# A decoder step with 32 experts: expert weights fetched in 2 MB pieces with 16 KB runs, and turns of the end part moved forward

## What is computed

```python
D_MODEL = D_FF = 1024; N_EXPERTS = 32; TOP_K = 4
SWIGLU_LIMIT = 7.0; SWIGLU_ALPHA = 1.702

def expert_block(args):            # xb: a block of the tokens of expert e
    xb, e = args
    gu = xb @ w_gu[e] + b_gu[e]    # w_gu[e] is 1024 x 2048: 8 MB
    gate, up = gu[:, :D_FF], gu[:, D_FF:]
    gate = jnp.minimum(gate, SWIGLU_LIMIT)
    up = jnp.clip(up, -SWIGLU_LIMIT, SWIGLU_LIMIT)
    hmid = (up + 1.0) * gate * jax.nn.sigmoid(SWIGLU_ALPHA * gate)
    return hmid @ w_down[e] + b_down[e]   # w_down[e] is 1024 x 1024: 4 MB
# y = for each token the sum of its 4 experts' rows, weighted by the gates
# x = x + y;  output = rmsnorm(x, norm_final)
```

## Time and profile before

| | |
|---|---|
| median of 3 runs | 1305.01 us (1304.98 to 1307.53) |
| the profiled execution's own time | 1306.43 us |
| its span, first to last instruction | 1304.7 us |
| granted TensorE clock, mean | 0.995 of full speed |
| bytes moved | 450.56 MB |
| experts' part, first bias matmul to the end | 355.25 to 1304.7 us |

### The profile page before, as it was taken

How to read it: one execution, slowest core, us unless ns; L and a number is a source line. 1 busy time by engine, 2 the same in 40 slices (tenths; PEclk the granted TensorE clock), 3 DMA queues, 4 the chain that set the end, 5 groups by cost and what they waited for, 6 DMA issues and landing times.

```text
span 1304.7 us, 19058 instructions
## 1 busy us (share of the span) xinstructions
PE 1258.8 (96%) x7105; PEld 544.9 (42%) x7105; DVE 474.7 (36%) x990; ACT 199.9 (15%) x347; POOL 65.2 (5%) x146
## 2 busy tenths in 40 slices
PE   7999989989899999999999999999999999999996
PEld 5887857655433333333333333333333333333321
DVE  1184776354553332222333222223333222222244
ACT  3223512222510000000000000000000000000002
POOL 3002102001300000000000000000000000000000
PEclk9999999999999999999999999999999999999998
DMA  9343307419689999999999999999999999999994
GB/s 302 130 154 131 115 6 245 161 52 361 257 340 404 422 422 422 422 422 422 422 422 422 422 421 422 422 422 422 422 422 422 422 422 422 422 422 422 422 422 186
DMA packets 87684, 450.56 MB, mean 345 GB/s; under 512 B 11746, under 2 KB 21080, under 8 KB 38392
## 3 DMA queue, kind: packets, MB, share of 16 engines
q1 hardware_dynamic: 82580, 446.18, 84.4%
q10 hardware_dynamic: 5068, 3.89, 1.2%
HBM read 443.88 MB, written 6.26 MB: 345 GB/s over the span
## 4 chain that ended last, share of the span: by engine, by line
PE 49%; DMA 16%; SPq 4%; DVE 1%; issue 0%; ACT 0%
PE ps L1012 22%; DMA ring<-in_w_gu 14%; PE ps L1038 14%; PE ps L985 6%; SPq L371 4%; PE ps L964 3%; DMA ring<-in_w_down 2%; PE ps L972 1%; PE ps L993 1%; PE ps L1002 1%; PE ps L1031 1%; PE ps L978 1%; DVE x_tok L1827 0%; DVE x_tok L1769 0%; SPq L381 0%
## 5 line engine op out<-in xcount | busy, mean ns | idle before, releaser
L1012 PE MATMUL ps<-ring,proj 128*64 128x512 f32 x2024 | 466.5, 598 | 6.9 <-DMA ring<-in_w_gu 6.3
L1038 PE MATMUL ps<-ring,proj 128*64 128x512 f32 x1024 | 245.7, 602 | 2.0 <-DMA ring<-in_w_down 1.6
L1012 PEld LDWEIGHTS ps<-ring,proj 128*64 128x64 f32 x2024 | 137.1, 137 | 254.4 <-issue 201.5
L1744 DVE TENSOR_SCALAR proj<-ps 128x512 f32<-128x512 f32 x32 | 22.1, 691 | 400.4 <-PE ps L1012 399.4
L1769 DVE TENSOR_TENSOR x_tok<-x_tok,ps 96x512 f32<-96x512 f32 x192 | 122.5, 678 | 98.6 <-PE ps L985 98.6
L1038 PEld LDWEIGHTS ps<-ring,proj 128*64 128x64 f32 x1024 | 64.9, 136 | 153.1 <-issue 146.5
L985 PE MATMUL ps<-proj 64*96 64x512 f32 x384 | 105.3, 627 | 0.6 <-DVE proj L1758 0.6
L615 PE MATMUL ps<-feat,ring 128*128 128x280 f32 x384 | 97.0, 404 | 0.0
L583 PE MATMUL ps<-feat,ring 128*128 128x280 f32 x384 | 93.2, 406 | 0.2 <-DVEq L1352 0.2
L583 PEld LDWEIGHTS ps<-feat,ring 128*128 128x128 f32 x384 | 74.0, 194 | 18.9 <-DVE feat L1351 0.5
L615 PEld LDWEIGHTS ps<-feat,ring 128*128 128x128 f32 x384 | 71.3, 191 | 19.5 <-issue 3.3
(11 more groups left out here) (361 smaller groups left out, 856.5 us busy)
## 6 DMA issues: line engine op xcount, KB each, us to landing
ring<-in_w_gu SPq DMA_DIRECT2D x253, 1024.0 KB, 24.3
ring<-in_w_down SPq DMA_DIRECT2D x128, 1024.0 KB, 23.4
ring<-in_w_in SPq DMA_DIRECT2D x11, 2048.0 KB, 9.1
ring<-in_w_in SPq DMA_DIRECT2D x2, 1024.0 KB, 9.1
out<-states SPq DMA_DIRECT2D x1, 2048.0 KB, 8.7
ring<-in_w_oa SPq DMA_DIRECT2D x1, 2048.0 KB, 7.7
ring<-in_w_ob SPq DMA_DIRECT2D x1, 2048.0 KB, 10.6
ring<-in_w_out SPq DMA_DIRECT2D x1, 2048.0 KB, 7.9
```

The costliest lines, as they stand in the source:

```text
L1012: last = mm(bank(j // 2)[64 * (j % 2):64 * (j % 2) + 64, :], xgT[:, k % 4, k // 4, :], w[:, 512 * j:512 * j + 512], start=False, stop=k == ...
L1038: last = mm(bank(4)[64 * j:64 * j + 64, :], hidT[:, k % 4, 64 * (k // 4):64 * (k // 4) + 64], ring[:, KT + k // 2, n:n + 512], start=False ...
L1744: ts(hid_g, bank(0), SWIGLU_LIMIT, None, ALU.min).then_inc(sg["gate_clipped"], 1)
```

## The change

1. From block 3 on one DMA fills two slots of gate/up (`gu_load2`): partition p gets rows 2p and 2p+1 of 256 rows, in one run of 16 KB. SP waits until both slots are used, PE waits at each even k for both. Blocks 0 to 2 keep single slots, but with the same assignment of rows (`gu_rows`).
2. Down is fetched by two DMAs of 2 MB; a partition gets four neighbouring rows, in one run of 16 KB. PE waits at k = 0 and k = 4, SP until two slots are used.
3. As the rows are spread otherwise, `turn_rows` reads every second column of `xg`, and `turn_hid` every fourth column of `hid`. The norm's weights come in the new order as `norm_pair` by a small DMA between the loads of `w_in`.
4. End part: in `down(nb-2)` `turn_share(nb-2)` stands after k = 1 and `turn_hid(nb-1)` after k = 5; `turn_share(nb-1)` stands ahead of `down(nb-1)`. Tiles of their own, `hidT_last` and `share_last`, take their results.
5. The last norm: for tiles 1 and 2 the second half of 512 columns is no longer DVE's. POOL multiplies it by `nfin_b`, ACT scales it by `rstd`.
6. Some semaphores are merged into counted ones (`mark`), with the same waits.

```diff
+            def gu_rows(e, q):
+                src = w_gu[0, e, 256 * q:256 * q + 256, :] if isinstance(e, int) else \
+                    w_gu[0][bass.ds(e, 1), 256 * q:256 * q + 256, :].rearrange("a p n -> (a p) n")
+                return src.rearrange("(p a) n -> p a n", a=2)
...
+            def gu_load2(e, q):
+                sp.dma_start(ring[:, 2 * q:2 * q + 2, :], gu_rows(e, q)).then_inc(w_arrived[2 * q], 16)
...
             def gu_loads(b, e):
-                for k in range(KT):
-                    sp.wait_ge(sg["gu_used"], GU0 + 8 * b - 8 + k + 1)
-                    gu_load(e, k)
+                for q in range(KT // 2):
+                    sp.wait_ge(sg["gu_used"], GU0 + 8 * b - 8 + 2 * q + 2)
+                    gu_load2(e, q)
...
             def down_loads(b, e):
-                for k in range(4):
-                    sp.wait_ge(sg["down_used"], DOWN0 + 4 * b - 4 + k + 1)
-                    down_load(e, k)
+                for q in range(2):
+                    sp.wait_ge(sg["down_used"], DOWN0 + 4 * b - 4 + 2 * q + 2)
+                    down_load(e, q)
...
                 for c in range(4):
-                    last = tr(turned[:, c, :], xg[:, 128 * c:128 * c + 128], ident[:])
+                    last = tr(turned[:, c, :], xg[:, 256 * (c // 2) + c % 2:256 * (c // 2) + 256:2], ident[:])
                 last.then_inc(sg["xg_turned"], 1)
...
                 for c in range(4):
-                    last = tr(hid_T[:, c, :], hid[:, 256 * (c // 2) + c % 2:256 * (c // 2) + 256:2], ident[:])
+                    last = tr(hid_T[:, c, :], hid[:, c::4], ident[:])
                 last.then_inc(sg["hid_turned"], 1)
...
-                    if k % 2 == 0:
+                    if k % 4 == 0:
                         pe.wait_ge(w_arrived[KT + k // 2], 16 * b + 32)
...
+                    if turns and k == 1:
+                        turn_share(b)
+                    if turns and k == 5:
+                        turn_hid(b + 1)
...
-            down(nb - 2, ())
-            turn_share(nb - 2)
-            turn_hid(nb - 1)
-            down(nb - 1, (0, 2, 4))
+            down(nb - 2, (), turns=True)
             turn_share(nb - 1)
+            down(nb - 1, h=hidT_last)
...
+            for i in range(1, NI):
+                pool.wait_ge(sg["comb_taken"], 6 * nb + COMB0 + 2 * i - 4)
+                pool.sem_inc(sg["wait_passed"], 1)
+                L.tell(gp.tensor_tensor(x_wtd[:, i - 1, :], x_tok[:, i, 512:D], nfin_b[:, 512:D], ALU.mult), "f_weighted", i)
...
+            for i in range(1, NI):
+                act.wait_ge(sg["f_root"], i + 1)
+                act.wait_ge(sg["f_weighted"], i)
+                L.tell(f(x_tok[:, i, 512:D], x_wtd[:, i - 1, :], ACT.Copy, scale=rstd[:, i:i + 1]), "f_rest", i)
```

More of the change, by code:

```diff
@@ L68, in hybrid_decoder_step @@
     X_ORDER = (1, 2, 0)
-    SMALL = 888
+    SMALL = 896
     DOWN0 = 16
@@ L195, in hybrid_decoder_step @@
         nbi = small(1, I32, 1)
+        norm_pair = small(KT)
         rt = [0]
@@ L279, in hybrid_decoder_step @@
             mark.update({name: (shared, n + 1) for n, name in enumerate(names.split())})
-        w_arrived = [sem(f"w_arrived{j}") for j in range(12)]
+        w_arrived = {j: sem(f"w_arrived{j}") for j in (0, 1, 2, 3, 4, 5, 6, 7, 8, 10)}
         class Steps:
@@ L330, in _ @@
                 if n == 5:
+                    sp.dma_start(norm_pair.rearrange("p (q a) -> p q a", a=2),
+                                 norm_ffn[0].rearrange("(q p a) -> p q a", p=128, a=2)).then_inc(sg["pair_norm_in"], 16)
                     sp.dma_start(w_rt[:], w_router[0].rearrange("(k p) n -> p k n", p=128)).then_inc(sg["route_in"], 16)
@@ L389, in _ @@
-            for k in range(4):
-                sp.sem_inc(w_arrived[KT + k], 16)
+                for q in range(2):
+                    sp.wait_ge(sg["down_used"], DOWN0 + 4 * b - 4 + 2 * q + 2)
+                    down_load(e, q)
+            for q in range(2):
+                sp.sem_inc(w_arrived[KT + 2 * q], 16)
             for k in range(4):
@@ L398, in _ @@
             sp.wait_ge(sg["conv_stored"], 144)
-            for k in range(4):
-                down_load(0, k)
+            for q in range(2):
+                down_load(0, q)
             sp.wait_ge(sg["mix_done"], 2 * NI)
@@ L984, in combine @@
                 for j in range(2):
-                    last = mm(bank(banks[j])[0:TP, :], share[64 * j:64 * j + 64, TP * i:TP * i + TP],
+                    last = mm(bank(banks[j])[0:TP, :], sh[64 * j:64 * j + 64, TP * i:TP * i + TP],
                               y_out[64 * j:64 * j + 64, :], start=True, stop=True)
@@ L992, in turn_hid, with gate_up @@
                 for c in range(4):
-                    last = tr(hid_T[:, c, :], hid[:, 256 * (c // 2) + c % 2:256 * (c // 2) + 256:2], ident[:])
+                    last = tr(hid_T[:, c, :], hid[:, c::4], ident[:])
                 last.then_inc(sg["hid_turned"], 1)
-            def gate_up(b, turn=False, share_of=None, next_rows=True, from_extra=False, add_of=None):
+            def gate_up(b, turn=False, share_of=None, next_rows=True, from_extra=False, add_of=None, paired=False):
                 pe.wait_ge(sg["xg_ready"], b + 1)
@@ L1025, in gate_up, with down @@
                         combine(6 * add_of + COMB0, k // 2 - 1)
-            def down(b, add_at=(0, 2, 4), banks=((5, 6),) * NI):
+            def down(b, add_at=(0, 2, 4), turns=False, h=hidT):
                 pe.wait_ge(sg["sel_dn_ready"], AHEAD + b + 1)
@@ L1065, in _ @@
             with pe.Fori(1, nb - 2) as b:
-                gate_up(b + 1, turn=True, share_of=b - 1)
+                gate_up(b + 1, turn=True, share_of=b - 1, paired=True)
                 turn_rows(b + 2)
                 down(b)
-            gate_up(nb - 1, turn=True, share_of=nb - 3, next_rows=False, add_of=nb - 3)
-            down(nb - 2, ())
-            turn_share(nb - 2)
-            turn_hid(nb - 1)
-            down(nb - 1, (0, 2, 4))
+            gate_up(nb - 1, turn=True, share_of=nb - 3, next_rows=False, add_of=nb - 3, paired=True)
+            down(nb - 2, (), turns=True)
             turn_share(nb - 1)
+            down(nb - 1, h=hidT_last)
             pe.wait_ge(sg["share_ready"], AHEAD + nb + 1)
@@ L1291, in sigmoid, with take_hidT @@
                 f(hid_s, hid_g, ACT.Sigmoid, scale=SWIGLU_ALPHA).then_inc(sg["sig_ready"], 1)
-            def take_hidT(b):
+            def take_hidT(b, out=hidT):
                 act.wait_ge(sg["hid_turned"], AHEAD + b + 1)
-                f(hidT, bank(3).rearrange("p (c t) -> p c t", c=4), ACT.Copy).then_inc(sg["hidT_ready"], 1)
+                f(out, bank(3).rearrange("p (c t) -> p c t", c=4), ACT.Copy).then_inc(sg["hidT_ready"], 1)
             def take_y(b):
@@ L1823, in _ @@
                 dve.wait_ge(sg["f_summed"], i + 1)
-                L(v.reciprocal(rstd[:, i:i + 1], rstd[:, i:i + 1]))
-                for j in range(2):
+                L.tell(v.reciprocal(rstd[:, i:i + 1], rstd[:, i:i + 1]), "f_root", i + 1)
+                for j in range(1 if i else 2):
                     half = slice(512 * j, 512 * j + 512)
                     L.tell(stt(out=x_tok[:, i, half], in0=x_tok[:, i, half], scalar=rstd[:, i:i + 1], in1=nfin_b[:, half],
-                               op0=ALU.mult, op1=ALU.mult), "f_ready", 2 * i + j + 1)
+                               op0=ALU.mult, op1=ALU.mult), "f_ready", i + j + 1 + (i > 0))
 _INS = ["x_prompt", "x_sample", "state_hgrn", "state_gdn", "state_conv", "meta_tokens", "lb_param", "norm_mix",
```

101 lines of the change are left out of this document (54 added, 47 removed).

## The result

| | before | after |
|---|---|---|
| median | 1305.99 us (1304.98 to 1307.53, 4 runs) | 1298.63 us (1298.34 to 1298.77, 4 runs) |
| ratio, 95% interval | | 0.9943 [0.9929, 0.9957] |
| span of the profiled execution | 1304.7 us | 1296.9 us |
| start of gate_up(31) | 1249.79 us | 1239.80 us |

The changed kernel is 0.57% faster. The forecast was 1310.3, slower; the time lies in the range, on the side of rival 1. Of the 10.0 us that the loop gained, the end part gave back 2.2.

The account below looks back on a forecast made before the run. PE was taken as the bound first, the transfers later. Faster transfers -12.7 us, turns +0.27 + 2.6 + 31 x 0.5 and the end -0.4 gave +5.3 on 1305.0: 1310.3 us, range 1294.5 to 1313.

Parts of the forecast that it names:

- rival 1: Stride four in `turn_hid` costs the same as stride two: 1295 us, or 1300 with 425 GB/s; chance 0.32.
- the cap of 12.7 us: Experts' loop: the most faster transfers can give up to the last block's start; beyond this PE is the bound.
- Runs of 16 KB: Weight loads: each run becomes one packet, rate 428 GB/s instead of 422, saving 12 us on the transfers' side.
- The turns: PE's transposes: new strides add 0.09 us a block in `turn_rows` and 0.50 in `turn_hid`; called the term that decides.
- x: Time per block that stride four adds in `turn_hid`: taken as 0.50 us, entering the sum 31 times.
- reading (a): Transposes' weight loads: time goes by the span of memory passed, so stride four adds 0.37 to 0.55 us a block; chance 0.50.
- The transfers' side in rival 1: Last landing 12 us earlier at 428 GB/s, down(31) waiting 6.1 us for 2 MB: in all about -10.8 us.
- Coarser pieces in the loop: Gate/up loads: half a slot less under way on average, one at most; cost put at nothing.
- The end: From down(30) to the last output: the end's terms sum to -0.4 us, give or take 1.
- the first weights of down(31): Ahead of down(31): its first 2 MB are issued late, so its first weights come 1.0 us later relative to down(30).
- the stretch from there to the last `combine`: Behind down(31): 1.1 us of turn and copy shrink to ACT's copy of the output, -0.3 us.
- the last norm: End of kernel: two halves of 0.77 us leave DVE, -1.5, but both last outputs are issued together, so -1.1 us.

Follow-up runs that it names:

- E6: The changed kernel with the four transposes of `turn_hid` done twice, result unchanged: 1312.42 us, ratio 1.0051 to the kernel before.
- E7: The changed kernel with one of the three parts of each row's sum left out in `pick_rows` (12 instead of 18 matmuls): 1298.82 us, ratio 0.9947.
- E1: The kernel before with the transposes' operands read at strides 1, 2, 3, 4, 8 and 16, output not the reference's: 1305.9 us (one run).
- E4: The changed kernel with 2 MB pieces kept but each run of 16 KB cut into two of 8 KB: 1311.9 us, ratio 1.0045.
- E9: The changed kernel with the last expert's down weights fetched in four pieces of 1 MB: 1295.78 us, ratio 0.9918 to the kernel before.
- E10: The changed kernel with the last norm on DVE alone, the last down still in 2 MB pieces: 1297.72 us, ratio 0.9942 to the kernel before.

## Why the prediction was wrong

**What bounds the kernel, and the cap of 12.7 us: right.** PE's block as measured is 28.92, and the start of gate_up(31) moved by 9.99 us. E6 shows that PE is the bound behind the cap, E7 that the transfers are close to it.

**Runs of 16 KB: right.** One packet per run, 428 GB/s as taken. With 8192 x 16 / 422 = 310.6 ns and 16384 x 16 / 428 = 612.5 ns per packet the fixed part is 8.7 ns (8.6 in the forecast). The estimate of 0.6%, by the 3 cycles of overhead that the Trainium skill gives (DMA: Bandwidth & Descriptors, Why small descriptors are slow), was too small: the trace has 1.4%.

**The turns: this step failed, and it turned the sign.** +0.09 for `turn_rows` was right (0.07). The x of `turn_hid` was put at 0.50 us per block and is 0: 209 ns a load before and after. The chosen reading (a), that a load's time goes by the span of memory passed, made a law out of two points, stride one and two, and the range of x was drawn inside that reading only. What the two points allowed was a slope or a switch, and E1 shows a switch: 195 ns at stride two, 206 at four, 197 at sixteen. 31 x 0.50 = 15.5 us of the sum were this term. With x = 0 the forecast's own formula gives -9.8 for the start of down(30), the profile -9.98. E6 shows that the rest of the step held: with 0.48 us really added the formula gives +5.1, the profile +3.7 (1272.59 against 1268.88), of which 0.6 is an earlier start of the experts' part and 0.6 the 29 x 0.02 of `turn_rows`. The rule of two hits per line of the Trainium skill (SBUF — State Buffer, Door 1: The DMA port swizzle), used for its direction, pointed the wrong way.

**The transfers' side in rival 1: right in kind.** -10.8 was worked out against -10.2 on PE's side, and after runs with both nearly equal: three short waits for gate/up, and no gain from less PE work in E7. Two sizes in it were off. PE goes on after down(30)'s last weights 12.96 us earlier (1263.50 against 1276.46; 12 forecast). But the first 2 MB of down(31) took 1271.29 - 1263.50 = 7.8 us from there, not the 6.1 put there; the forecast itself read 7.7 for 2 MB in its part on the end.

**Coarser pieces in the loop, "nothing": right.** Where PE is the bound, nothing is seen. In E4, where the transfers are in the later part, as many bytes move from 495 to 1240 us as before; its loss is in the main at the end.

**The end: mis-sized, -0.4 forecast, +2.2 measured** (from -9.98 at down(30) to -7.8 at the end). Three terms of it:
- the first weights of down(31): +1.0 forecast, +1.2 measured (9.98 - 8.79). Right.
- the stretch from there to the last `combine`: -0.3 forecast, +0.5 measured. The second 2 MB arrive late too (0.46 us of waiting); the forecast looked at the first only. In E9, without that wait, the stretch is 0.2 us shorter than before (11.50 against 11.67).
- the last norm: -1.1 forecast, +0.5 measured. The forecast took 0.77 us for each of DVE's halves as if POOL ran beside it at no cost; 0.89 us went there. Of the hoped-for -1.5 DVE kept -0.67 (from the last `combine` to its last result 9.31 us in after, 9.98 in E10), and that went in the output: in E10 the first of the last two transfers is issued while DVE still works, 9.22 us after the `combine`, in after both are issued from 9.33 on, and SP is done with them later, 10.58 against 10.32. E10's rows, with its last `combine` at 1282.68:

```profile
1291.13 1.53 DVE L1846 SCALAR_TENSOR_TENSOR x_tok<-x_tok,sm,proj 96x512 f32<-96x512 f32 x2
1291.90 1.10 SPq L453 DMA_DIRECT2D out<-x_tok  x2
```

**The sum with the terms as measured.** 1305.0 - 9.98 + 2.2 = 1297.2. The kernel before came out at 1305.99 in the later comparison, 1.0 above the three runs that the forecast started from; from there it is 1298.2, for 1298.63 measured. Rival 1 with 428 GB/s, 1295, misses by its end part and this one microsecond.

**The chances.** The argument for rival 1 stood in the text: the shortest load at stride two, 194 ns, is close to exactly half speed, and two strides aren't a law. It got 0.32, against 0.50 for a reading that rested on nothing more. With a term of 31 times x that decides the sign and no row for it, the two readings should have been given about the same weight.

## What to carry to other kernels

A cost seen at two settings gives a slope or a switch; if its multiple decides the sign, forecast both with even weight, and measure a third setting first (one run with a stride of its own per instruction is enough). In this loop pieces of 2 MB cost nothing, but the last fetch, behind which nothing stands in the queue, should stay fine: 1 MB pieces instead of 2 MB were worth 3 us. A share of the work given to a second engine at the end can slow the first one (here by 0.89 us), and its gain has to be counted to the issue of the last output, not to the first engine's last instruction.

## What the runs showed of the hardware

- Weight loads of 128 x 128 f32 take 138 ns at stride one and 195 to 206 ns at strides 2, 3, 4, 8 and 16 (E1; 209 in before at stride two and in after at two and four).
- The rate by length of a run is 390, 417, 422 and 428 GB/s for 2, 4, 8 and 16 KB. A line of 8.6 ns per packet and 0.0368 ns per byte, drawn through 2 and 8 KB, meets 16 KB too; at 4 KB it would give 411.
- 2 MB pieces with runs of 8 KB (E4) moved 314.33 MB in 745 us, 1 MB pieces with the same runs (before) 314.32.
- A DVE multiplication that began under one of POOL's took 1640 ns instead of 748.
